# Expert value products on one Trainium2 core: which operand is held, which one passes, and what the last stage has left to turn

## The chip, the cores and the metric

The kernel runs on one core of one Trainium2 chip. The metric is device time in microseconds (us). TensorE (PE) multiplies: a weight load puts a 128x128 tile into its array (the operand that is held), and a matmul passes the columns of the other operand through it into PSUM.
## The reference

One decoder layer for 512 prompt tokens and 64 sample tokens, 2048 wide: a mixer, then a layer that retrieves experts, then a last norm. The change lies behind the mixer. Of the experts it matters that the second table `v_tab` has 128 x 128 rows of 2048, and that the layer adds to each token the sum of 128 chosen rows, each by its weight:

```python
u = u_tab[eidx]
act = jax.nn.gelu(jnp.einsum('thkd,td->thk', u, xb).astype(jnp.float32), approximate=False)
return jnp.einsum('thk,thkd->td', (gate * act).astype(xb.dtype), v_tab[eidx])
...
out = lax.map(one_block, hb).reshape(Tp, D)[:T].reshape(B, L, D)
return x + out.astype(x.dtype)
...
y_prompt = rmsnorm(hp, w_norm_final)
y_sample = rmsnorm(hs, w_norm_final)
```

## The kernel before, in words

The token rows are five tiles: 0 to 3 are the prompt, and tile 4 holds the 64 sample tokens. Tile 0 and tile 4 fetch their chosen expert rows from memory one by one ("gathered"). Tiles 1 to 3, 384 tokens (`ND`), are computed densely: for them every one of the 16384 expert rows is multiplied, with a weight that is zero where an expert was not chosen. Dense products are made in three passes to keep float32 accuracy: each operand is split into a high and a low part, and high x high, high x low and low x high are added up in PSUM.

The stage "hidden" makes the experts' activations from the first table. The stage `outputs` then multiplies the weights (activation times gate) by the second table, and `finish` adds the residual `sums` (what the mixer left) and does the last norm.

In `outputs` the table comes in 128 units of 1 MB (`un`, tiles units_raw, units_whi, units_wlo), eight units to a chunk, 16 chunks. A chunk is 8 x 128 experts; for each chunk the weights of all 384 tokens are loaded (`load_chunk`, two transfers of 1.5 MB, tile units_big), multiplied (`weigh`) and split (`weights_hi`, `weights_lo`; tiles outputs_w_hi and outputs_w_lo, two buffers). The order on every engine is written out by hand in a `body` for two chunks, of which the middle ones run in a hardware loop (`turns`). Per unit j of a chunk:

- SP loads unit n + 2 into one of two raw buffers, once DVE has split unit n. At j = 0 it then issues the next chunk's two weight loads. One queue carries all of these in order.
- ACT splits off the high part of unit n + 1 (L1522), once TensorE is done with unit n - 1. DVE makes the low part (L1526) behind it.
- DVE also weighs the next chunk (L2139, L2146), adds PSUM results to the accumulator `acc` (L2157, L2159), and takes one gathered row (even j) or two (odd j) into `accg` (L2170). POOL issues the gathers into three row buffers.
- PE waits for the low part of unit n, then runs 48 matmuls. The value unit is held, 128 of its columns at a time, and the 384 tokens' weights pass. So a PSUM tile is 128 features x 384 tokens, and `acc` comes out with the features on partitions: transposed.

`finish` therefore loads tiles of `sums`, turns `acc` back with 48 transposes on PE (L2278), adds them on DVE (L2315), and does the norm tile by tile in the order 0, 1, 4, 2, 3: a square with its sum on ACT (L2291), a root (L2293), a Newton step of five small operations on DVE, and the scaling (L2327).

## Time and profile before

| | us |
|---|---|
| median of 3 runs (3772.39 to 3776.6) | 3774.61 |
| the profiled execution's own time | 3772.87 |
| its span in the trace | 3771.1 |
| stage `outputs`, from its first matmul to its last one's end | 2663.9 to 3733.0 |
| `finish`, to the end of the span | 3735.8 to 3771.1 |

The span is what the trace covers, 1.8 us less than the execution's own time. A matmul's duration in the trace is its way through the array, which overlaps with that of the next one; the pace is the distance between two starts.

### The profile page before, as it was taken

The page shows a single profiled execution, that of the slowest core. Times are in us where ns is not written, and L with a number is a line of the kernel's source. Part 1 is how long each engine was busy: PE and PEld are TensorE (multiplying, and loading weights), DVE is VectorE, ACT ScalarE, POOL GpSimd, SP SyncE.
Part 4 walks back from the last instruction along what each step waited for, and adds up shares of the span by engine and source line. Part 5 has one row for each costly group of instructions (what it writes and reads, how often), then busy time and mean ns, then how long its engine had stood idle before and what let it go on. Part 6 is the DMA issues. An engine that isn't in the chain of part 4 may idle for free. (4 is left out here: it accounts for less than half of the span.)

```text
span 3771.1 us, 50107 instructions
## 1 busy us (share of the span) xinstructions
PE 3548.6 (94%) x19479; PEld 3301.7 (88%) x19479; DVE 2556.0 (68%) x3619; ACT 1286.4 (34%) x1610; POOL 920.3 (24%) x609
## 2 busy tenths in 40 slices
PE   8999999776997999999999999999799999999996
PEld 6888887555786878999999999999799999999996
DVE  4112221786323216999999888887889899898987
ACT  5112221332322213323325777774222222222222
POOL 0000000000000000032333333333355445454552
PEclk9999999676998999999999999999899999999998
DMA  5223320542623405487888999999898999989986
GB/s 207 87 111 111 114 106 29 190 148 92 227 90 133 154 35 203 161 327 293 318 332 314 375 372 374 385 372 386 334 376 345 377 362 356 369 350 376 358 344 250
DMA packets 186998, 965.63 MB, mean 256 GB/s; under 512 B 18657, under 2 KB 61345, under 8 KB 86098
## 3 DMA queue, kind: packets, MB, share of 16 engines
q1 hardware_dynamic: 108082, 506.07, 35.6%
q0 software_dynamic: 61264, 426.27, 29.0%
q10 hardware_dynamic: 17488, 31.06, 2.3%
q8 instruction: 108, 1.77, 0.2%
q14 instruction: 56, 0.46, 0.0%
HBM read 865.77 MB, written 97.55 MB: 255 GB/s over the span
## 5 line engine op out<-in xcount | busy, mean ns | idle before, releaser
L1754 PE MATMUL hidden_hp<-dense_hi,units_whi 128*128 128x384 f32 x2048 | 697.4, 341 | 24.1 <-DVE units_wlo L1526 24.1
L1755 PE MATMUL hidden_hp<-dense_lo,units_whi 128*128 128x384 f32 x2048 | 688.0, 336 | 0.0
L1756 PE MATMUL hidden_hp<-dense_hi,units_wlo 128*128 128x384 f32 x2048 | 687.9, 336 | 0.0
L2234 PE MATMUL outputs_vp<-outputs_w_hi,units_whi 128*128 128x384 f32 x2032 | 679.0, 334 | 0.9 <-DVE units_wlo L1526 0.9
L2236 PE MATMUL outputs_vp<-outputs_w_hi,units_wlo 128*128 128x384 f32 x2032 | 678.7, 334 | 0.0
L2235 PE MATMUL outputs_vp<-outputs_w_lo,units_whi 128*128 128x384 f32 x2032 | 678.7, 334 | 0.0
L1522 ACT CAST units_whi<-units_raw 128x2048 fp32r<-128x2048 f32 x214 | 410.7, 1920 | 774.0 <-PE outputs_vp L2236 631.7
L1696 POOL DMA_INDIRECT hidden_row<-u_rows,expert_ids x192 | 360.7, 1878 | 1037.8 <-DVE dots L1977 656.8
L1526 DVE TENSOR_TENSOR units_wlo<-units_raw,units_whi 128x2048 fp32r<-128x2048 f32 x214 | 489.9, 2290 | 117.7 <-ACT units_whi L1522 116.3
L2170 DVE SCALAR_TENSOR_TENSOR accg<-outputs_row,outputs_w_op,accg 128x2048 f32<-128x2048 f32 x192 | 450.8, 2348 | 52.0 <-DMA outputs_row<-v_rows,outputs_id 49.2
L1977 DVE CUSTOM_DVE_ANT_0 hidden_row<-hidden_row,hidden_h_row 128x2048 f32<-128x2048 f32 x192 | 435.7, 2287 | 58.6 <-DMA hidden_row<-u_rows,expert_ids 57.8
L2032 POOL DMA_INDIRECT outputs_row<-v_rows,outputs_id x192 | 320.4, 1669 | 526.4 <-DVE accg L2170 477.8
L1754 PEld LDWEIGHTS hidden_hp<-dense_hi,units_whi 128*128 128x128 f32 x2048 | 387.7, 189 | 29.2 <-DVE units_wlo L1526 28.9
L1755 PEld LDWEIGHTS hidden_hp<-dense_lo,units_whi 128*128 128x128 f32 x2048 | 387.7, 189 | 0.0
L1756 PEld LDWEIGHTS hidden_hp<-dense_hi,units_wlo 128*128 128x128 f32 x2048 | 387.1, 189 | 0.0
L2234 PEld LDWEIGHTS outputs_vp<-outputs_w_hi,units_whi 128*128 128x128 f32 x2032 | 381.4, 188 | 1.9 <-issue 1.2
L2235 PEld LDWEIGHTS outputs_vp<-outputs_w_lo,units_whi 128*128 128x128 f32 x2032 | 381.4, 188 | 0.0
L2236 PEld LDWEIGHTS outputs_vp<-outputs_w_hi,units_wlo 128*128 128x128 f32 x2032 | 381.4, 188 | 0.0
L543 PE MATMUL in_proj_acc<-in_proj_whi,in_proj_rows_hi 128*128 128x512 f32 x960 | 376.2, 392 | 1.9 <-DVE in_proj_wlo L436 1.9
L549 PE MATMUL in_proj_acc<-in_proj_whi,in_proj_rows_lo 128*128 128x512 f32 x768 | 299.5, 390 | 0.0
L548 PE MATMUL in_proj_acc<-in_proj_wlo,in_proj_rows_hi 128*128 128x512 f32 x768 | 299.5, 390 | 0.0
L1828 ACT ACTIVATE hidden_hid<-hidden_hp 128x384 f32<-128x384 f32 x128 | 63.0, 492 | 570.7 <-PE hidden_hp L1756 561.8
(358 smaller groups left out, 4825.2 us busy)
## 6 DMA issues: line engine op xcount, KB each, us to landing
units_raw<-v_units SPq DMA_DIRECT2D x128, 1024.0 KB, 7.2
units_raw<-u_units SPq DMA_DIRECT2D x86, 1024.0 KB, 7.5
in_proj_raw<-w_in SPq DMA_DIRECT2D x48, 1024.0 KB, 5.5
hidden_raw<-u_units SPq DMA_DIRECT2D x42, 1024.0 KB, 7.7
hidden<-hidden_hid SPq DMA_DIRECT2D x128, 192.0 KB, 4.3
gate_mat<-units_big SPq DMA_DIRECT2D x12, 2048.0 KB, 21.6
units_big<-hidden SPq DMA_DIRECT2D x16, 1536.0 KB, 10.1
units_big<-gate_mat SPq DMA_DIRECT2D x16, 1536.0 KB, 15.9
```

The lines of the kernel that those rows point to most:

```text
L543: nc.tensor.matmul(acc[t][:], hi_at(t, kk), whi[q][:, k, :], start=first, stop=False)
L1522: self.nc.scalar.copy(self.hi[s][:], self.raw[raw][:]).then_inc(self.hi_done, 1)
L1526: self.nc.vector.tensor_tensor(self.lo[s][:], self.raw[self.slot(n, s)][:], self.hi[s][:].bitcast(F32), ALU.subtract).then_inc(self.lo_don ...
L1696: pool.indirect_dma_start(row[g % U_ROWS][:], None, u_rows, bass.IndirectOffsetOnAxis(expert_ids[:, g:g + 1], 0)).then_inc(row_in[g % U_RO ...
L1754: mm(o, un.hi[s][:, x, :], h_hi[:, x, :], start=x == 0, stop=False)
L1755: mm(o, un.hi[s][:, x, :], h_lo[:, x, :], start=False, stop=False)
L1756: ins = mm(o, un.lo[s][:, x, :], h_hi[:, x, :], start=False, stop=x == KT - 1)
L1977: v.tensor_tensor_reduce(r[:], r[:], h_row[g % 3 // 2][:], 1.0, 0.0, mult, ALU.add, dots[:, g:g + 1]).then_inc(row_used, 1)
L2170: v.scalar_tensor_tensor(o[:], r[:], w_op[:, j:j + 1], o[:], mult, ALU.add).then_inc(gat.row_used, 1)
L2234: mm(o, un.hi[x][:, at, :], W_hi[s][:, e, :], start=e == 0, stop=False)
L2235: mm(o, un.hi[x][:, at, :], W_lo[s][:, e, :], start=False, stop=False)
L2236: ins = mm(o, un.lo[x][:, at, :], W_hi[s][:, e, :], start=False, stop=e == CH - 1)
```

## The change

The operands of the second table's products change places. The tokens' weights are held (128 tokens x 128 experts), and 512 columns of values pass. A unit is now 4 x 128 experts by 512 features, two units make a group (8 x 128 experts), and each group fills three PSUM tiles, one for each token tile, in token order. DVE adds a group's three tiles in one go at the following even unit. `acc` is three tiles of token rows; they begin as the rows of `sums`, which SP loads at the start of the stage, and the table is laid out anew in memory to match. `finish` has no transposes and no loads of `sums`, and it does the norm in three batches of tiles: 0, then 1 and 2, then 3 and 4. A half of a chunk's weights is now enough for its first unit. The lines shown are the diff without the bookkeeping of names.

```diff
@@ outputs
+        def group(i, s, g):
+            return DS // 2 * (2 * i + s) + g
...
             sp.dma_start(accg[1][0:NSMP, :], sums[SEQ:SEQ + NSMP, :]).then_inc(sums_in, 16)
+            for t in range(VT):
+                sp.dma_start(acc[t][:], sums[P * (t + 1):P * (t + 2), :]).then_inc(acc_in, 16)
             turns(sp, body, T)
-            sp.dma_start(X[:], sums[P:2 * P, :]).then_inc(early, 16)
-            sp.wait_ge(early, 16)
...
-            def add(i, s, j, b):
-
-                k = DT * unit(i, s, j) + b
-                vec.wait_ge(un.done, NKEYS + k + 1)
...
+            def add(i, s, g, t):
+
+                k = VT * group(i, s, g) + t
+                vec.wait_ge(un.done, NKEYS + 2 * VT * group(i, s, g) + VT + t + 1)
+                if isinstance(i, int) and i == s == g == t == 0:
+                    vec.wait_ge(acc_in, 16 * VT)
+
+                wait(vec, added, k + 1 - VT * DS // 2)
+                o = acc[t][:, NB * g:NB * (g + 1)]
+                v.tensor_tensor(o, o, vp[(VT * (DS // 2 * s + g) + t) % 8][:], ALU.add).then_inc(added, 1)
...
-                        add(i, s, j, 0)
+                        if j % 2 == 0:
+                            add_ahead(i, s, j)
                         for x in range(3 * (DS * s + j) // 2, 3 * (DS * s + j + 1) // 2):
                             gathered(i, x)
-                        add(i, s, j, 1)
+                        if is_last(i, s) and j == DS - 1:
+                            for t in range(VT):
+                                add(i, s, DS // 2 - 1, t)
...
-                        for b in range(DT):
-
-                            wait(pe, added, DT * (n - 4) + b + 1)
-                            o = vp[DT * (j % 4) + b][:, 0:ND]
-                            for e in range(CH):
-                                at = DT * e + b
-                                mm(o, un.hi[x][:, at, :], W_hi[s][:, e, :], start=e == 0, stop=False)
-                                mm(o, un.hi[x][:, at, :], W_lo[s][:, e, :], start=False, stop=False)
-                                ins = mm(o, un.lo[x][:, at, :], W_hi[s][:, e, :], start=False, stop=e == CH - 1)
+                        if j < 2:
+                            pe.wait_ge(w_lo_done, 2 * (2 * i + s) + j + 1)
+                        for t in range(VT):
+                            if h == 0:
+
+                                wait(pe, added, VT * group(i, s, j // 2) + t + 1 - 8)
+                            o, at = vp[(VT * (DS // 2 * s + j // 2) + t) % 8], slice(P * t, P * (t + 1))
+                            for e in range(HC):
+                                w = (slice(None), HC * h + e, at)
+                                v_hi, v_lo = (u[x][:, 4 * e:4 * e + 4, :].rearrange("p k f -> p (k f)") for u in (un.hi, un.lo))
+                                mm(o[:], W_hi[s][w], v_hi, start=h == e == 0, stop=False)
+                                mm(o[:], W_hi[s][w], v_lo, start=False, stop=False)
+                                ins = mm(o[:], W_lo[s][w], v_hi, start=False, stop=h == 1 and e == HC - 1)
                             ins.then_inc(un.done, 1)
@@ finish
-        @block.tensor
-        def _(pe):
-            for t in range(1, PTILES):
-                for b in range(4):
...
-                        ins = nc.tensor.transpose(bank[g % 8][:, k, :], acc[:, 4 * b + k, (t - 1) * P:t * P], ident[:])
...
+        batches = [(0, 1), (1, 3), (3, TILES)]
...
-            for n in range(1, TILES):
-                add(order[n])
-                norm(n - 1)
-            norm(TILES - 1)
+            norm(0)
+            add_half()
+            norm(1)
+            norm(2)
@@ kernel
-        "v_units": put("v_units", v.reshape(NCH, CH, NKEYS, DS, DT * P).transpose(0, 3, 2, 1, 4).reshape(NCH * DS, P, D)),
+        "v_units": put("v_units", v.reshape(NCH, 2, CH // 2, NKEYS, D // NB, NB).transpose(0, 4, 1, 3, 2, 5).reshape(NCH * DS, P, D)),
```

On VectorE, units 2 and 3 of the first chunk stood so before. units_wlo is a unit's low part, units_big the weighing of the next chunk, acc the addition of a PSUM tile outputs_vp, and accg a gathered row:

```order
L1526 TENSOR_TENSOR units_wlo1<-units_raw1,units_whi1 128x2048
L2139 TENSOR_TENSOR units_big0<-units_big0,units_big1 128x384 x2
L2157 COPY acc<-outputs_vp4 128x384
L2170 SCALAR_TENSOR_TENSOR accg0<-outputs_row0,outputs_w_op,accg0 128x2048
L2157 COPY acc<-outputs_vp5 128x384
L1526 TENSOR_TENSOR units_wlo0<-units_raw0,units_whi0 128x2048
L2139 TENSOR_TENSOR units_big0<-units_big0,units_big1 128x384 x2
L2157 COPY acc<-outputs_vp6 128x384
L2170 SCALAR_TENSOR_TENSOR accg0<-outputs_row1,outputs_w_op,accg0 128x2048
L2170 SCALAR_TENSOR_TENSOR accg1<-outputs_row2,outputs_w_op,accg1 128x2048
L2157 COPY acc<-outputs_vp7 128x384
```

The same two units with the change:

```order
L1527 TENSOR_TENSOR units_wlo1<-units_raw1,units_whi1 128x2048
L2143 TENSOR_TENSOR units_big0<-units_big0,units_big1 128x384 x2
L2162 TENSOR_TENSOR acc0<-acc0,outputs_vp0 128x512
L2162 TENSOR_TENSOR acc1<-acc1,outputs_vp1 128x512
L2162 TENSOR_TENSOR acc2<-acc2,outputs_vp2 128x512
L2186 SCALAR_TENSOR_TENSOR accg0<-outputs_row0,outputs_w_op,accg0 128x2048
L1527 TENSOR_TENSOR units_wlo0<-units_raw0,units_whi0 128x2048
L2143 TENSOR_TENSOR units_big0<-units_big0,units_big1 128x384 x2
L2186 SCALAR_TENSOR_TENSOR accg0<-outputs_row1,outputs_w_op,accg0 128x2048
L2186 SCALAR_TENSOR_TENSOR accg1<-outputs_row2,outputs_w_op,accg1 128x2048
```

Four additions of 384 columns, one on each side of the gathered rows, became three of 512 columns in the even unit. The last addition of an odd unit, which stood between its gathered rows and the next unit's low part, is gone.

On SyncE, at the start of the stage, these transfers stood one behind the other before:

```order
L2088 DMA accg0<-sums 128x2048
L2089 DMA accg1<-sums 64x2048
L1514 DMA units_raw0<-v_units 128x2048
L1552 DMA units_big0<-hidden 128x3072
L1553 DMA units_big1<-gate_mat 128x3072
L1514 DMA units_raw1<-v_units 128x2048
```

With the change:

```order
L2092 DMA accg0<-sums 128x2048
L2093 DMA accg1<-sums 64x2048
L2095 DMA acc0<-sums 128x2048
L2095 DMA acc1<-sums 128x2048
L2095 DMA acc2<-sums 128x2048
L1515 DMA units_raw0<-v_units 128x2048
L1553 DMA units_big0<-hidden 128x3072
L1554 DMA units_big1<-gate_mat 128x3072
L1515 DMA units_raw1<-v_units 128x2048
```

Three loads of 1 MB now stand ahead of unit 2 (the first units_raw), of the next chunk's weights and of unit 3 (the second units_raw).

## Rows read from the trace of the kernel before

**Rows 1.** Page, costliest groups: a matmul of `outputs`; count, busy, mean ns, idle before

```profile
L2234 PE MATMUL outputs_vp<-outputs_w_hi,units_whi 128*128 128x384 f32 x2032 | 679.0, 334 | 0.9 <-DVE units_wlo L1526 0.9
```

**Rows 2.** Busy time, granted clock (PEclk), DMA share and GB/s by stretch

```profile
core 0: us, PE busy (x) PEld busy (x) DVE busy (x) ACT busy (x) POOL busy (x), PEclk, DMA share, GB/s
2663.90:2674.30 10.40, 10.40 (x48) 10.40 (x49) 7.61 (x9) 3.27 (x2) 0.00 (x0) 0.78 1.02 423
2674.30:3732.80 1058.50, 1057.59 (x6098) 1056.50 (x6096) 949.26 (x729) 282.68 (x156) 533.15 (x374) 1.00 0.90 356
```

**Rows 3.** Timeline of PE, 384 columns: start us, us; 57 starts listed

```profile
2999.70 0.33 PE L2235 MATMUL outputs_vp<-outputs_w_lo,units_whi 128*128 128x384 f32 x1
...
3009.41 0.33 PE L2234 MATMUL outputs_vp<-outputs_w_hi,units_whi 128*128 128x384 f32 x1
```

**Rows 4.** Timeline of PE in the input projection, 512 columns; 28 starts listed

```profile
299.67 0.39 PE L548 MATMUL in_proj_acc<-in_proj_wlo,in_proj_rows_hi 128*128 128x512 f32 x1
...
305.79 0.39 PE L548 MATMUL in_proj_acc<-in_proj_wlo,in_proj_rows_hi 128*128 128x512 f32 x1
```

**Rows 5.** Timeline of ACT at the stage's start; bracket: idle before, and releaser

```profile
2686.19 1.91 ACT L1522 CAST units_whi<-units_raw 128x2048 fp32r<-128x2048 f32 x1 [9.60 <-DMA units_raw<-v_units]
2691.32 1.91 ACT L1522 CAST units_whi<-units_raw 128x2048 fp32r<-128x2048 f32 x1 [3.22 <-PE outputs_vp L2236]
```

**Rows 6.** Timeline of DVE, and DMA use by stretch, at the stage's start

```profile
2688.14 2.29 DVE L1526 TENSOR_TENSOR units_wlo<-units_raw,units_whi 128x2048 fp32r<-128x2048 f32 x1 [3.58 <-ACT units_whi L1522]
...
2664.00:2692.00 28.00, 28.00 (x150) 28.00 (x151) 20.75 (x20) 7.77 (x5) 6.62 (x6) 0.92 1.01 421
```

**Rows 7.** Around a wait of PE in the stage before: timeline row, and stretch behind it

```profile
1741.75 1.11 PE L1713 MATMUL hidden_tq<-ident,units_big 128*128 128x128 f32 x4 [3.69 <-DMA units_big<-queries]
...
1742.00:1746.00 4.00, 4.00 (x15) 4.00 (x15) 3.60 (x8) 2.38 (x2) 0.24 (x1) 0.50 1.02 422
```

**Rows 8.** Timeline of a steady chunk: SP and ACT

```profile
3262.06 0.33 SPq L1514 DMA_DIRECT2D units_raw<-v_units  x1
...
3285.15 1.92 ACT L1522 CAST units_whi<-units_raw 128x2048 fp32r<-128x2048 f32 x1 [8.95 <-DMA units_raw<-v_units]
3290.93 1.92 ACT L1522 CAST units_whi<-units_raw 128x2048 fp32r<-128x2048 f32 x1 [3.86 <-PE outputs_vp L2236]
```

**Rows 9.** Timeline of the same chunk: DVE

```profile
3287.46 2.28 DVE L1526 TENSOR_TENSOR units_wlo<-units_raw,units_whi 128x2048 fp32r<-128x2048 f32 x1
...
3290.60 0.55 DVE L2159 TENSOR_TENSOR acc<-acc,outputs_vp 128x384 f32<-128x384 f32 x1
3291.06 2.34 DVE L2170 SCALAR_TENSOR_TENSOR accg<-outputs_row,outputs_w_op,accg 128x2048 f32<-128x2048 f32 x1
...
3309.51 2.29 DVE L1526 TENSOR_TENSOR units_wlo<-units_raw,units_whi 128x2048 fp32r<-128x2048 f32 x1 [0.59 <-ACT units_whi L1522]
...
3326.15 2.29 DVE L1526 TENSOR_TENSOR units_wlo<-units_raw,units_whi 128x2048 fp32r<-128x2048 f32 x1 [0.77 <-ACT units_whi L1522]
```

**Rows 10.** Waits in the stage: engine line waited for, us in total, times, longest

```profile
ACT units_whi L1522 <- DMA units_raw<-v_units: 129.3, 15, 9.6
DVE accg L2170 <- DMA outputs_row<-v_rows,outputs_id: 49.2, 28, 4.2
```

**Rows 11.** Timeline of DVE in the last unit of `outputs` and in `finish`

```profile
3734.04 0.55 DVE L2159 TENSOR_TENSOR acc<-acc,outputs_vp 128x384 f32<-128x384 f32 x1
...
3743.17 2.27 DVE L2307 TENSOR_TENSOR accg<-accg,finish_half 64x2048 f32<-64x2048 f32 x1
3745.37 0.14 DVE L2321 TENSOR_SCALAR finish_mean<-finish_ss 128x1 f32<-128x1 f32 x1
...
3746.81 2.35 DVE L2327 SCALAR_TENSOR_TENSOR sums<-sums,finish_rstd,finish_w 128x2048 f32<-128x2048 f32 x1
3749.08 2.47 DVE L2315 TENSOR_TENSOR finish_x<-finish_x,finish_t 128x512 f32<-128x512 f32 x4
...
3762.69 2.35 DVE L2327 SCALAR_TENSOR_TENSOR finish_x<-finish_x,finish_rstd,finish_w 128x2048 f32<-128x2048 f32 x1
```

More of the change, by code:

```diff
@@ L61 @@
 DS = D // (DT * P)
+VT = PTILES - 1
 NGATHER = HK + HK // 2
@@ L2038, in wait_row, with outputs @@
         return self.row[j % ROWS]
-def outputs(nc, name, un, big, w_in, v_units, hidden, G, v_rows, expert_ids, dots, acc, accg, sums, X, early):
+def outputs(nc, name, un, big, w_in, v_units, hidden, G, v_rows, expert_ids, dots, acc, accg, sums):
     mult = ALU.mult
@@ L2200, in _ @@
             mm = nc.tensor.matmul
-            def first_unit():
-                for h in range(2):
-                    pe.wait_ge(w_lo_done, h + 1)
-                    for b in range(DT):
-                        o = vp[b][:, 0:ND]
-                        for e in range(HC * h, HC * (h + 1)):
-                            at = DT * e + b
-                            mm(o, un.hi[0][:, at, :], W_hi[0][:, e, :], start=e == 0, stop=False)
-                            mm(o, un.hi[0][:, at, :], W_lo[0][:, e, :], start=False, stop=False)
-                            ins = mm(o, un.lo[0][:, at, :], W_hi[0][:, e, :], start=False, stop=e == CH - 1)
-                        if h == 1:
-                            ins.then_inc(un.done, 1)
             def body(i):
@@ L2218, in body @@
                     for j in range(DS):
-                        n = unit(i, s, j)
+                        n, h, x = unit(i, s, j), j % 2, j % 2
                         un.ready(pe, NKEYS + n)
-                        if j == 0 and not (isinstance(i, int) and i == s == 0):
-                            pe.wait_ge(w_lo_done, 2 * (2 * i + s + 1))
-                        x = j % 2
-                        if isinstance(i, int) and i == s == j == 0:
-                            first_unit()
-                            continue
@@ new lines, in body @@
+                        for t in range(VT):
+                            if h == 0:
[7 more added lines that the diff above has]
+                                ins = mm(o[:], W_lo[s][w], v_hi, start=False, stop=h == 1 and e == HC - 1)
@@ L2302, in _, with add_half @@
             v, d = nc.vector, Steps(vec, dstep)
[L2304 to L2315 removed]
+            def add_half():
+                t = PTILES
+                vec.wait_ge(moved, 1)
+                v.tensor_tensor(X[t][0:NSMP, :], X[t][0:NSMP, :], half[:], ALU.add).then_inc(summed, 1)
@@ L2317, in norm @@
             def norm(n):
[L2318 to L2321 removed]
+                lo, hi = batches[n]
+                at = slice(lo, hi)
+                vec.wait_ge(squared, hi)
+                v.tensor_scalar(mean[:, at], ss[:, at], 1.0 / D, EPS, ALU.mult, ALU.add).then_inc(meaned, 1)
                 vec.wait_ge(meaned, n + 1)
@@ L2323, in norm @@
                 vec.wait_ge(rooted, n + 1)
-                newton_rsqrt(nc, d, rstd[0:R, at], mean[0:R, at], root[0:R, at], tmp[0:R, at])
+                newton_rsqrt(nc, d, rstd[:, at], mean[:, at], root[:, at], tmp[:, at])
                 if n == 0:
                     vec.wait_ge(w_in, 16)
-                v.scalar_tensor_tensor(X[t][0:R, :], X[t][0:R, :], rstd[0:R, at], W[0:R, :], ALU.mult,
-                                       ALU.mult).then_inc(done, 1)
-            for n in range(1, TILES):
-                add(order[n])
-                norm(n - 1)
@@ L2333, in _ @@
-            norm(TILES - 1)
+                for t in range(lo, hi):
+                    R = tile_rows(t)
+                    v.scalar_tensor_tensor(X[t][0:R, :], X[t][0:R, :], rstd[0:R, t:t + 1], W[0:R, :], ALU.mult,
+                                           ALU.mult).then_inc(done, 1)
+            norm(0)
+            add_half()
+            norm(1)
+            norm(2)
 def build(nc, x, w, consts, keys, tables, states, outs):
@@ L2362, in build @@
                            w["norm_ffn"], expert_ids, dots, gates0, G)
-        acc, accg = sb("acc", [P, KT, ND]), [sb(f"accg{x}", [P, D]) for x in range(2)]
-        X, early = sb("sums1", [P, D]), shared.sem("sums_early")
-        outputs(nc, "outputs", un, big, w_in, tables["v_units"], hidden, G, tables["v_rows"], expert_ids, dots, acc, accg, sums, X, early)
-        finish(nc, "finish", ident, sums, w["norm_final"], acc, accg, X, outs["y"])
+        acc, accg = [sb(f"acc{t}", [P, D]) for t in range(VT)], [sb(f"accg{x}", [P, D]) for x in range(2)]
+        outputs(nc, "outputs", un, big, w_in, tables["v_units"], hidden, G, tables["v_rows"], expert_ids, dots, acc, accg, sums)
+        finish(nc, "finish", w["norm_final"], acc, accg, outs["y"])
 def kernel(**inputs):
```

83 lines of the change are left out of this document (32 added, 51 removed).

## Prediction

> **What bounds the kernel now.** I read the page first, then busy time by stretch, then timelines. In `outputs` TensorE is busy from its first matmul to its last: 1057.6 of 1058.5 us at full clock behind the first unit, and its matmuls waited 0.9 us in all for the value units [rows 1, 2]. So the stage's time is the number of matmuls times the distance between two starts. That distance, and not the 334 ns that the page gives as a mean, is the price of a matmul: 57 starts in a row lie 9.71 us apart, 9.71 / 56 = 173.4 ns for 384 columns [rows 3]. 6144 of them make 1065.3 us.
>
> What is close behind matters as much. The DMA engines are busy 0.90 of the stage at 356 GB/s, and VectorE 949.3 of 1058.5 us [rows 2]. Once in each chunk, 15 times, ScalarE waits for a value unit to land and not for TensorE [rows 10]. It is unit 3, which stands in SP's queue behind the next chunk's weights. In the chunk shown it landed at 3285.15, its low part was made from 3287.46 to 3289.74, and TensorE came to it at about 3290.7 (ScalarE is let go at 3290.93, when the last matmul of unit 2 ends, and the next matmul starts some 0.2 us ahead of that end) [rows 8, 9]: 1.0 us to spare. At the stage's start it was 2690.43 against 2691.1 by the same reading, 0.7 us [rows 5, 6].
>
> **Matmuls: -20.8 us.** The change makes 16 chunks x 4 feature blocks x 3 token tiles x 8 x 3 passes = 4608 matmuls of 512 columns in place of 6144 of 384. The columns passed are the same. What falls is what each matmul costs beyond its columns. The trace has 128x512 matmuls of the same types in the input projection, where 28 starts lie 6.12 us apart: 226.7 ns [rows 4]. 4608 x 226.7 = 1044.5 us, against 1065.3. The two prices fit one line of 0.416 ns a column plus 13.5 ns a matmul, and 1536 x 13.5 = 20.8. A unit takes 8.16 us in place of 8.32, a chunk 65.3 in place of 66.6.
>
> The Trainium skill, page "TensorE: Matmul & The Clock Gate", section "Back-to-back issue gap", gives columns / 2.4 + 2.5 ns for an isolated matmul at full clock. By it 512 columns cost 215.8 ns and 384 cost 162.5, and the change would bring 998.4 - 994.4 = 4 us. The rows have 11 ns more at either width, so the trace's prices are taken.
>
> **The loads at the stage's start: +7.4 us, and +1.7 for the clock.** Three loads of 1.05 MB now stand in SP's queue ahead of units 2 and 3. From 2664 to 2692 the DMA engines are full at 421 GB/s [rows 6], so 3.15 MB more push what stands behind by 7.5 us. Unit 3 landed at 2686.2 [rows 5]; it will land near 2693.7, and its low part is there at about 2697.9. TensorE, which started at 2663.9 and needs 10.3 us for the cold first unit and 8.16 for each of the next two, wants it at 2690.5. It waits about 7.4 us, in two parts, because unit 2 stands behind the same loads. Who is queued behind it: nothing but TensorE's own units, since VectorE and ScalarE wait for the same landing. A wait of 3.7 us in the stage before was followed by 4 us at the 1.2 GHz level, with 15 matmul starts where 23 would fit at full pace [rows 7]: 8 x 0.173 = 1.4 us. For one wait of that kind or a little more I take 1.7. Bounds of the whole term: 0, if the gathers give way to the loads and the slack is larger than I read, and 7.4 + 2 x 2 = 11.4.
>
> **The loop through VectorE and the DMA queue: +6 us.** This term decides how much of the gain is kept. From the issue of unit 2 to the landing of unit 3 it is 3262.06 to 3285.15, 23.1 us [rows 8], nearly all full DMA engines. Then 2.0 us for the high part. From the start of unit 3's low part to the end of that of the next chunk's unit 0, which lets SP issue the next unit 2, it is 3287.46 to 3328.44, 41.0 us, with 0.59 + 0.77 us of idle time [rows 9]: 39.6 us of work. The change alters it: ten additions of 384 columns at a cadence of 0.46 us (3290.60 to 3291.06 [rows 9]) become nine of 512 at 0.62 (four in 2.47 [rows 11]), 5.6 for 4.65, so 40.5. The addition ahead of unit 3's low part is gone, so this starts at the high part's end. The loop is then 23.1 + 2.0 + 40.5 = 65.6 us, against 66.6 that TensorE took for a chunk and 65.3 that it will take. What had 1 us to spare now lacks 0.3. The slack of 1.0 us is used up in a few chunks (0.5 of it goes at once, since TensorE gets to unit 3 sooner), and then each chunk waits about 0.3: some 4 us over 12 chunks. Landings scatter by about 1 us from chunk to chunk, and a late one now stops TensorE: 2 more. Bounds: 0, and 1 us in each of 15 chunks, 15 us. VectorE's total is unchanged: a chunk had 16 additions at 0.46 and has 12 at 0.62, 7.4 us either way. The PSUM tiles are no bound: a tile is wanted again eight tiles, over two groups, later.
>
> **The end of the stage: -0.9 us.** VectorE's last addition began at 3734.04, 1.1 us behind the last matmul, because two gathered rows stood ahead of it [rows 11]. Now they come before TensorE is done, and one addition of 0.7 us is left.
>
> **Finish: -7.4 us.** Its first scaling still waits for the norm's weights, so it ends at the same distance, 3743.25, and the sample tile's addition at 3745.44 [rows 11]. Then comes one small chain of 1.44 us (3745.37 to 3746.81), two scalings of 2.35, again 1.44 and two scalings: 3745.37 + 12.3 = 3757.7. Before, the last scaling ended at 3765.04. The two additions of 2.47 us and two of four small chains on the path are gone: 4.94 + 2.9 = 7.8, less half a us of waits that differ. ScalarE's squares (1.9 us each) lie beside the scalings. The transposes stood beside other work and bring nothing.
>
> **Sum.** -20.8 + 7.4 + 1.7 + 6 - 0.9 - 7.4 = -14.0 us against the profiled execution's 3772.87: 3758.9. That execution is 1.7 us below the median of the runs; I split the difference and say 3760.
>
> **The rivals.** (A) The start's loads are hidden and no chunk waits: 3760 - 9.1 - 6 = 3745. For it speaks that both waits hang on 1 us of slack or less, carried over to another schedule; against it, full DMA engines at the start. (B) The loop is dearer, about 1 to 1.9 us a chunk: 3767 to 3782. For it, the rows' landings, for which VectorE already waits 49.2 us, up to 4.2 at once [rows 10]; they stand in the same full stretch. Against it, the DMA engines would be busy 0.90 x 66.6 / 65.3 = 0.92, and idle time makes up for delays. (C) Slower: the wait at a chunk's unit 3 grows to 3.7 us, at which the clock has fallen once [rows 7]. Each such chunk costs 3.7 + 1.7 = 5.4 us; from the forecast, 4 such chunks give 3782 and all 15 give 3841. It decides from a landing 3 us later than now. (D) A matmul of 512 columns costs the same per column here as one of 384, 231.2 ns, and nothing is saved on TensorE: 3781. Only another cost for these operands would do it, as the row of 512 columns says otherwise [rows 4]. By the skill's formula it would be 4 us and not 20.8 that is saved, which gives 3777; it has a share of D's chance.
>
> **How the numbers follow.** Forecast 0.56, with its own range of 3751 to 3767; A 0.15, B 0.17, C 0.05, D and the formula 0.07. A measurement of this kernel can tell about 0.2%, 7.5 us, from no change, so faster means below 3767.1 and slower above 3782.2. The forecast and A are faster but for a little of the upper edge, and B's lower end is too: 0.74. Same takes the rest of B and D: 0.18. Slower is C and the ends of B and D: 0.08. The range of 8 in 10 reaches down to A and up to B's middle: 3745 to 3774.
>
> **What would show it.** Right: starts of 226.7 ns in `outputs`; a first wait of PE for units_wlo of some 7 us in all before unit 3, and the clock at 1.2 GHz behind it; PE waits of 0.2 to 1 us once in a chunk at unit 3; VectorE's waits for ScalarE at units 5 and 7 gone; `finish` 28 us long in place of 35. Wrong: no waits at all (A), PE waits above 1 us in each chunk (B), granted clock below 1.00 in the steady stretch (C), or starts of about 231 ns (D).

## The result, and the profile after

The change made the kernel slower. Median 3806.65 us of 4 runs (3794.0 to 3811.45) against 3775.57 of 4 runs of before (3772.39 to 3776.6): ratio 1.0077, 95% interval 1.006 to 1.0095 (the ratios here and below are worked out from all runs, and can differ a little from that of two medians). The forecast was 3760, and the range ended at 3774. The profiled execution is the lowest of the four, 3794.0 with a span of 3792.2, so the traces explain 21.1 us of span (3792.2 - 3771.1); the 12.7 us from it to the median lie in runs that have no trace. All runs of this document show about the same granted clock, 0.95 to 0.96, but one of e11's ten (3851.53 us at 0.90), which its ratio leaves out; without it e11's median is 3776.98.

The waits of the stage (engine line waited for, us in total, times, longest), to be held against [rows 10]. Of GpSimd's wait for a row buffer, before's line stands first:

```profile
POOL outputs_row L2032 <- DVE accg L2170: 477.8, 103, 14.7
```

```profile
POOL outputs_row L2033 <- DVE accg L2186: 563.7, 133, 14.7
...
ACT units_whi L1523 <- DMA units_raw<-v_units: 263.5, 34, 14.1
DVE accg L2186 <- DMA outputs_row<-v_rows,outputs_id: 67.9, 35, 4.4
...
PE outputs_vp L2236 <- DVE units_wlo L1527: 31.3, 10, 4.5
```

ScalarE waits for a unit's landing 34 times in place of 15, and TensorE, which waited 0.9 us for low parts [rows 1], waits 31.3. Busy time by stretch (columns as in [rows 2]), from the first matmul to unit 3 and from there to the stage's end:

```profile
2667.60:2701.80 34.20, 29.73 (x109) 23.86 (x110) 17.74 (x14) 7.08 (x4) 4.97 (x6) 0.83 1.01 422
2701.80:3762.40 1060.60, 1033.79 (x4501) 851.10 (x4499) 933.89 (x661) 278.82 (x154) 482.73 (x368) 0.99 0.88 348
```

The DMA engines moved 348 GB/s over the long stretch, less than before (356 in [rows 2]), and the granted clock is no longer 1.00. The span's 21.1 us add up so: the stages ahead of `outputs` ended 3.7 us later (2667.6 against 2663.9; this start lay anywhere from 2660.0 to 2670.5 in the runs below and is no effect of the change). From the first matmul to unit 3 it is 34.2 us in place of 27.2, +7.0. From unit 3 to the last matmul's end it is 1060.6 in place of 1041.9 (2691.1 to 3733.0), +18.7. From there to the end of the span it is 29.8 (3762.4 to 3792.2) in place of 38.1, -8.3. Together 21.1.

So the start and the end of the stage can be read off at once (+7.0 and -8.3), and the loss is in the long stretch. One of its chunks, on TensorE:

```profile
3039.61 0.39 PE L2237 MATMUL outputs_vp<-units_wlo,outputs_w_hi 128*128 128x512 f32 x1
...
3042.56 0.39 PE L2238 MATMUL outputs_vp<-units_whi,outputs_w_lo 128*128 128x512 f32 x1
3045.14 0.50 PE L2236 MATMUL outputs_vp<-units_whi,outputs_w_hi 128*128 128x512 f32 x1 [2.19 <-DVE units_wlo L1527]
```

14 starts lie 2.95 us apart, 2.95 / 13 = 226.9 ns, as forecast. Then unit 3's low part is not there. Why it is not shows in the timelines of the same chunk, SP and ACT first, then DVE:

```profile
3015.38 0.33 SPq L1515 DMA_DIRECT2D units_raw<-v_units  x1
...
3040.85 1.91 ACT L1523 CAST units_whi<-units_raw 128x2048 fp32r<-128x2048 f32 x1 [12.27 <-DMA units_raw<-v_units]
```

```profile
3042.79 2.29 DVE L1527 TENSOR_TENSOR units_wlo<-units_raw,units_whi 128x2048 fp32r<-128x2048 f32 x1 [2.71 <-ACT units_whi L1523]
...
3045.94 1.87 DVE L2162 TENSOR_TENSOR acc<-acc,outputs_vp 128x512 f32<-128x512 f32 x3
3047.73 2.34 DVE L2186 SCALAR_TENSOR_TENSOR accg<-outputs_row,outputs_w_op,accg 128x2048 f32<-128x2048 f32 x1
...
3080.69 2.28 DVE L1527 TENSOR_TENSOR units_wlo<-units_raw,units_whi 128x2048 fp32r<-128x2048 f32 x1
```

Issue of unit 2 to landing of unit 3: 25.5 us, where [rows 8] had 23.1. High part 1.9. Start of unit 3's low part to the end of that of the next unit 0: 3042.79 to 3082.97, 40.2, with no idle time. The loop is 67.6 us and TensorE needs 65.3. The fence also shows the new order: three additions in a block (1.87 us), and only then the gathered row. Before, one addition of 0.46 stood there [rows 9].

What a wait leads to is seen behind three of them, the one above and these two:

```profile
2908.09 0.80 PE L2236 MATMUL outputs_vp<-units_whi,outputs_w_hi 128*128 128x512 f32 x1 [4.04 <-DVE units_wlo L1527]
...
3113.83 0.80 PE L2236 MATMUL outputs_vp<-units_whi,outputs_w_hi 128*128 128x512 f32 x1 [3.10 <-DVE units_wlo L1527]
```

Busy time in the 8.2 or 8.3 us behind each, in order of time:

```profile
2908.10:2916.40 8.30, 8.30 (x30) 6.77 (x31) 8.30 (x10) 1.90 (x1) 2.44 (x2) 0.81 0.43 154
...
3045.20:3053.40 8.20, 8.20 (x36) 6.79 (x37) 8.20 (x10) 1.91 (x1) 2.43 (x2) 1.00 0.53 208
...
3113.80:3122.00 8.20, 8.17 (x24) 6.50 (x25) 8.20 (x10) 1.90 (x1) 2.43 (x2) 0.65 0.48 190
```

### The profile page after: what moved, and what is told of

Same layout as the page of the kernel before. It is cut to its first block and busy times, and to the rows that moved or that the text cites. A ratio compares the mean times of both kernels' runs of the same rounds, so it can differ in the third digit from the quotient of the medians.

```text
span 3792.2 us, 46689 instructions
## 1 busy us (share of the span) xinstructions
PE 3538.7 (93%) x17895; PEld 3104.8 (82%) x17895; DVE 2540.0 (67%) x3531; ACT 1286.0 (34%) x1608; POOL 873.5 (23%) x609
## 5 line engine op out<-in xcount | busy, mean ns | idle before, releaser
L2236 PE MATMUL outputs_vp<-units_whi,outputs_w_hi 128*128 128x512 f32 x1536 | 606.0, 395 | 53.8 <-DVE units_wlo L1527 31.3
L2237 PE MATMUL outputs_vp<-units_wlo,outputs_w_hi 128*128 128x512 f32 x1536 | 603.4, 393 | 0.0
L2238 PE MATMUL outputs_vp<-units_whi,outputs_w_lo 128*128 128x512 f32 x1536 | 603.1, 393 | 0.0
L2033 POOL DMA_INDIRECT outputs_row<-v_rows,outputs_id x192 | 338.8, 1765 | 595.6 <-DVE accg L2186 563.7
L2236 PEld LDWEIGHTS outputs_vp<-units_whi,outputs_w_hi 128*128 128x128 f32 x1536 | 292.1, 190 | 119.9 <-DVE units_wlo L1527 36.2
L2237 PEld LDWEIGHTS outputs_vp<-units_wlo,outputs_w_hi 128*128 128x128 f32 x1536 | 292.4, 190 | 60.9
L2238 PEld LDWEIGHTS outputs_vp<-units_whi,outputs_w_lo 128*128 128x128 f32 x1536 | 291.8, 190 | 61.4
```

The lines of the kernel that those rows point to most:

```text
L2236: mm(o[:], W_hi[s][w], v_hi, start=h == e == 0, stop=False)
L2237: mm(o[:], W_hi[s][w], v_lo, start=False, stop=False)
L2238: ins = mm(o[:], W_lo[s][w], v_hi, start=False, stop=h == 1 and e == HC - 1)
```

## The experiments

Fourteen kernels ran, in four groups, each group beside its own runs of before (medians 3775.24, 3777.17, 3774.64 and 3776.0). The legs of the loop are worked out from the timelines of DVE and ACT as in the chunk above, as the mean of 14 chunks. "DMA leg" is the end of unit 0's low part (SP then issues unit 2) to the start of unit 3's high part, "high" from there to the start of its low part, "VectorE" from there to the end of the next unit 0's low part. Rows and SP are the MB that the gathers' queue and SP's moved in the DMA leg; POOL is how long GpSimd waited for a row buffer, and how often; the last column is TensorE's waits for low parts.

```
                                median   ratio, 95%               DMA leg rows SP   high VectorE  chunk  POOL waits  PE waits
before                          3775.57                             23.4  3.82 5.76  2.5   40.8    66.7  477.8, 103    0.9
after                           3806.65  1.0077 (1.0060, 1.0095)    25.5  4.58 5.96  2.0   40.7    68.2  563.7, 133   31.3
e3  no loads at the start       3793.22  1.0041 (1.0027, 1.0055)    26.2  4.69 6.09  1.9   40.5    68.7  563.5, 133   36.7
e4  weights behind unit 3       3831.16  1.0150 (1.0133, 1.0167)    19.9  3.75 3.46  3.3   47.6    70.7  596.8, 130   57.8
e5  gates behind unit 3         3767.83  0.9979 (0.9969, 0.9988)    20.4  3.76 4.59  4.3   41.7    66.4  550.1, 136   13.4
e6  e5, residual last           3771.03  0.9988 (0.9976, 0.9999)    20.2  3.76 4.56  4.1   41.9    66.2  535.2, 132   13.0
e7  short additions             3755.55  0.9946 (0.9930, 0.9963)    23.2  3.97 5.86  2.1   40.1    65.4  508.0,  91    5.8
e8  additions spread            3784.19  1.0021 (1.0010, 1.0031)    25.6  4.66 5.98  2.0   39.8    67.4  470.8, 106   28.0
e9  row, then additions         3775.15  0.9999 (0.9989, 1.0009)    24.5  4.66 5.69  2.0   40.2    66.7  464.4,  91   20.4
e10 e9 and e5                   3754.26  0.9944 (0.9927, 0.9961)    20.1  3.75 4.75  4.3   40.9    65.3  474.1,  89    4.5
e12 e10, residual last          3753.35  0.9942 (0.9925, 0.9959)    20.2  3.71 4.85  4.2   40.9    65.3  478.6,  92    2.1
e11 before, VectorE filled      3778.01  1.0011 (1.0001, 1.0021)    23.3  3.91 5.67  2.6   41.0    66.9  425.8, 108    3.5
e13 before, block ahead of row  3795.50  1.0051 (1.0034, 1.0068)    24.8  4.30 5.90  2.0   40.9    67.6  557.7, 137    8.7
e14 before, row ahead of block  3780.20  1.0012 (1.0002, 1.0021)    24.7  4.64 5.75  2.0   40.4    67.0  477.2,  92    3.7
```

**Are the matmuls cheaper? e1 and e2**: both kernels without the gathered rows, the queue and VectorE relieved.

```diff
@@ POOL
-            turns(pool, body, T)
@@ DVE, gathered
-                v.scalar_tensor_tensor(o[:], r[:], w_op[:, j:j + 1], o[:], mult, ALU.add).then_inc(gat.row_used, 1)
```

> The changed kernel with the gathered rows left out of the stage (neither fetched nor added, so tile 0 and the sample tile lack their experts). It is to price the matmuls alone. Theory of the loop (DMA queue and VectorE at a chunk's start): a third of the DMA bytes and half of VectorE's work are gone, TensorE waits only at the start, starts 226.7 ns apart, from first to last matmul 128 x 8.16 + 2 = 1047 us, up to 1053 with the start's loads. Rival, dearer matmuls in this place: above 1060 us though nothing waits.

> The kernel before with the gathered rows left out in the same way. Both theories: starts 173.4 ns apart, from first to last matmul 128 x 8.32 + 2 = 1067 us. Against e1_no_rows this is the matmul term by itself: 20.5 us between the two stages if the term is right, less than 5 if held weights cost per column what they did.

One run each: 3738.76 and 3777.05. From the first matmul's start to the last one's it is 1046.6 us (e1) and 1067.0 (e2), a difference of 20.4, where the term had 20.8. So the matmuls are cheaper by what was forecast. In after the gain is there too, and waits outweigh it.

**The loads at the start: e3.** The first chunk's results are copied, and the sums are not loaded.

```diff
-            for t in range(VT):
-                sp.dma_start(acc[t][:], sums[P * (t + 1):P * (t + 2), :]).then_inc(acc_in, 16)
...
+                if isinstance(i, int) and i == s == 0:
+                    v.tensor_copy(o, vp[(VT * g + t) % 8][:]).then_inc(added, 1)
```

> The changed kernel without the three loads of the residual at the stage's start: the first chunk's additions are copies, so tiles 1 to 3 lack the residual. Theory of the loop: TensorE reaches unit 3 some 27 us behind its first matmul and not 34, and the time falls by 7 to 8 us; the waits of the later chunks stay. Rival, the loads set off the later waits too (a backlog that is carried on from chunk to chunk): it falls by 20 us or more. Rival, nothing hangs on the loads: within 2 us.

Unit 3 begins 27.3 us behind the first matmul in place of 34.1, so the loads cost 6.8 there. The loop does not get shorter (68.7 us a chunk, PE waits 36.7), and from first to last matmul start the two traces are level, 1094.4 us. The medians lie 13.4 us apart, between the 7 to 8 and the 20 that were given ahead, so the size of the effect on the time stays open (the runs of after alone scatter over 17 us). Either way e3 is slower than before: the loads can explain a part of the loss and not its direction.

**The weights' place in SP's queue: e4 and e5.** The two loads of 1.5 MB for the next chunk stand between units 2 and 3. e4 issues both one unit later, e5 only the second (gate_mat).

```diff
@@ e4
-                        if j == 0 and not is_last(i, s):
+                        if j == 1 and not is_last(i, s):
                             load_w(2 * i + s + 1)
@@ e5
-                        if j == 0 and not is_last(i, s):
-                            load_w(2 * i + s + 1)
+                        if j < 2 and not is_last(i, s):
+                            load_w(2 * i + s + 1, j)
```

> The changed kernel with the next chunk's two weight loads issued one unit later, behind unit 3 in SP's queue and not ahead of it; nothing else. Theory of the loop: unit 3 lands 7 us sooner, the wait at unit 3 goes, VectorE may then wait a little for the weights at unit 2; the time falls by 25 to 40 us, to 3765 to 3780. Rival, the DMA engines' total is the limit: the same bytes, within 5 us. Rival, VectorE's total work is the limit: within 5 us as well.

> The changed kernel with one of the next chunk's two weight loads, that of the gates (gate_mat, 1.5 MB), issued behind unit 3; the other stays ahead of it. Theory of the loop, as the traces of the changed kernel show it (23 to 28 us, on the mean 25.5, from the issue of unit 2 to the landing of unit 3, 1.9 for the high part, 40.2 on VectorE, 68 in all): 1.57 MB fewer ahead of unit 3 are 3.7 to 6.5 us, the loop falls below TensorE's 65.3 us for a chunk, the waits at unit 3 go: 25 to 43 us less than the changed kernel, 3763 to 3780. In the former run with both loads behind unit 3 VectorE stood 5 us a chunk for them; here the queue never runs dry, so it should wait under 1.5. Rival, the DMA engines' total is the limit: within 5 us of the changed kernel, near 3805.

e4 was a miss, 24.5 us above after where 25 to 40 less had been expected, and told something. The DMA leg fell to 19.9 us, but the wait went to VectorE, which now stood before an operand that had not landed, with the low parts of all later units queued behind it:

```profile
DVE units_big L2143 <- DMA units_big<-gate_mat: 69.1, 14, 6.0
```

Its leg grew by 7 us. e5 keeps the first load early, has nearly the same short DMA leg and only 1 us more on VectorE, and gets 38.8 us below after, as expected (VectorE's waits for gate_mat are 3.1 us in all). So what is bought in the queue counts only up to the next operand that is wanted.

**The start's loads once more: e6** is e5 with the residual loaded in the last chunk into the free weight tiles, and added there.

```diff
+                        if j == 0 and is_last(i, s):
+                            sp.wait_ge(w_lo_done, 2 * NCH)
+                            for t in range(VT):
+                                sp.dma_start(spare[t], sums[P * (t + 1):P * (t + 2), :]).then_inc(acc_in, 16)
...
+                v.tensor_tensor(acc[t][:], acc[t][:], spare[t], ALU.add).then_inc(resid, 1)
```

> As e5_gates_behind_unit3, and the residual is not loaded at the stage's start: the first chunk's additions are copies, and in the last chunk, which has no weights to load or to weigh, the three tiles of the residual are loaded into the room of the weights and added by VectorE. Theory: 7 to 9 us less than e5_gates_behind_unit3, 3755 to 3770, below the kernel before. Rival: VectorE's three additions of 2.3 us in the last chunk make TensorE wait, and it is level with e5_gates_behind_unit3.

The stage's first to last matmul start fell by 2.7 us (1069.9 to 1067.2), yet the median is not below e5's, and the intervals overlap; 7 to 9 us less had been expected. The trace shows that the stall moved: in the last chunk unit 3 now stands behind the three residual loads, ScalarE waits 17.26 us for it to land, and TensorE then 7.23 us for its low part (3692.55), the longest wait of its stage.

**How long the additions are: e7, and where they stand: e8.** e7 adds 64 columns of the 512. e8 puts one of the three ahead of the even unit's row, one behind it and one into the odd unit.

```diff
@@ e7
-                o = acc[t][:, NB * g:NB * (g + 1)]
+                o = acc[t][:, NB * g:NB * g + 64]
@@ e8
-                        if j % 2 == 0:
-                            add_ahead(i, s, j)
+                        add_ahead(i, s, j - j % 2, (2,) if j % 2 else (0,))
                         ...
+                        if j % 2 == 0:
+                            add_ahead(i, s, j, (1,))
```

> The changed kernel with each of VectorE's additions cut to 64 of 512 columns (tiles 1 to 3 lack most of the products). It takes VectorE's part of the loop down and leaves DMA alone. Theory of the loop: nine additions in the VectorE leg at 0.2 and not 0.62 us, the leg falls from 40.2 to about 36.5, the loop from 68.2 to 64.4, below TensorE's 65.3, so most of the waits go: 25 to 40 us less than the changed kernel. Rival, DMA's total or the burst alone sets the wait, and VectorE does not: within 5 us.

> The changed kernel with the same three additions of a group, but spread: one ahead of an even unit's gathered row, one behind it, one in the odd unit. Work is the same, only the place differs. Theory of the order (the three additions in a block move the gathers' issues into the stretch in which unit 3 is loaded): the DMA leg goes back to 23.3 us, the loop to about 65, and 30 us or more are won. Theory of the coupling (once the loop is longer than TensorE's chunk, whatever makes it so, the backlog grows into it): no more than the 0.6 us by which the VectorE leg gets shorter, 9 us at most over 15 chunks.

With short additions all of the gain is there, 51 us below after; but this takes work from VectorE and time from ahead of the row together. It did not come the way that was expected either. VectorE's leg was to fall to 36.5 us and stayed at 40.1, now with some 3.9 us of idle time, since a chunk can't be shorter than TensorE's 65.3; what fell is the DMA leg, from 25.5 to 23.2. With the same work in other places, e8 is 22 us below after. That is neither of the figures given ahead of it, but it says that the place is part of the cause. Its DMA leg is as long as after's (25.6); what fell is GpSimd's waits and VectorE's leg.

**The place alone: e9**, the same three additions right behind the row. **e10** joins it with e5.

```diff
-                        if j % 2 == 0:
-                            add_ahead(i, s, j)
                         for x in range(3 * (DS * s + j) // 2, 3 * (DS * s + j + 1) // 2):
                             gathered(i, x)
+                        if j % 2 == 0:
+                            add_ahead(i, s, j)
```

> The changed kernel with one order turned round: in an even unit VectorE takes the gathered row first and then makes the three additions. The same work. It moves the issue of the last gather ahead of unit 2's load from 1.4 to 2.0 us before it to some 3.3 us before it (2.7 in the kernel before, 3.4 in e7_short_additions, where the DMA leg was 23.2 us). Theory of the place (a gather issued right ahead of unit 2 shares the queue's stretch and costs its bytes there): DMA leg 23.5 us, loop 65.7, 25 to 35 us less than the changed kernel, 3770 to 3780. Rival, only idle time of VectorE helps, which spreads all the gathers: the DMA leg stays above 25, less than 10 us are won.

> e9_rows_then_additions and e5_gates_behind_unit3 together. Theory: in e5 the chunk takes 66.4 us because the rows' landings and the gates hold VectorE; the earlier gather takes up to 1 us of that, 3755 to 3765. Rival: VectorE's waits for the gates stay what they are, level with e5 (3768).

Two lines that swap places are worth some 30 us: 31.5 between the medians, 29 by the two ratios, each of which has its own runs of before. The time is as expected, the leg only in part: GpSimd's waits for a row buffer fall from 563.7 to 464.4 us, the DMA leg from 25.5 to 24.5 (23.5 was expected), the chunk from 68.2 to 66.7 (65.7). What went are the long legs. Over the 14 chunks of after they run from 23.2 to 27.6 us, and eight are longer than the longest of e9, where they run from 23.5 to 25.1 (before: 22.4 to 24.9). In e10 the loop takes 65.3 us, what TensorE needs, and of TensorE's idle time only what lies at the start is left (page, costliest groups):

```profile
L2238 PE MATMUL outputs_vp<-units_whi,outputs_w_hi 128*128 128x512 f32 x1536 | 599.7, 390 | 26.9 <-DVE outputs_w_lo L2152 22.3
```

Of the 26.9 us of idle time, 22.3 lie ahead of the stage's first matmul, and 4.5 are the start's wait for unit 2. In after the same row reads:

```profile
L2236 PE MATMUL outputs_vp<-units_whi,outputs_w_hi 128*128 128x512 f32 x1536 | 606.0, 395 | 53.8 <-DVE units_wlo L1527 31.3
```

**Or is it VectorE's lost idle time? e11** leaves before's order and gives VectorE three memsets of 512 columns in each chunk.

```diff
+                        if j in (3, 4, 6):
+                            v.memset(spare[:], 0.0)
```

> The kernel before with three clears of a spare 128x512 tile added to VectorE in units 3, 4 and 6 of each chunk, some 1.3 us a chunk, just about the idle time that it has there; matmuls are as before. If the DMA leg is fixed, the loop is 23.3 + 2.0 + 40.9 = 66.2 us, below TensorE's 66.6, and the time stays within 4 us. If VectorE's idle time is what keeps the gathers apart from unit 2's load, the DMA leg grows to 25 or more, the loop to 68, and the kernel before becomes 15 to 30 us slower, though TensorE has no less time for a chunk than it had.

The DMA leg stayed (23.3), and the time rose by 0.11% (0.01 to 0.21). A VectorE that is fuller by this much does not lengthen the transfers by itself. One of the three fillings stands ahead of the last row that is taken before unit 2's load, but it is 0.48 us long, where the block of after is 1.87.

**All three: e12**, which is e10 with e6's residual.

> e10_rows_first_gates_late with the residual added in the last chunk as in e6_and_residual_last. Theory: 6 us less than e10, 3748 to 3760. Rival: as e6 was level with e5 or 3 us above it, the start's stall only moves, and it is level with e10.

3753.35 us, 0.9942 of before: the best kernel of the study, no different from e10 within the intervals. Its stage takes 1048.7 us from first to last start, 4.9 less than e10's, and as in e6 there is a wait of TensorE in the last chunk, of 2.13 us.

**The order without the change: e13 and e14.** The old matmuls and the old `finish`, but four additions of 384 columns in a block at even units, ahead of the row (e13) or behind it (e14).

```diff
+            def add_ahead(i, s, j):
+                for y in (j - 2, j - 1):
                     ...
+                    for b in range(DT):
+                        add(*back, b)
...
-                        add(i, s, j, 0)
+                        if j % 2 == 0:
+                            add_ahead(i, s, j)
                         for x in range(3 * (DS * s + j) // 2, 3 * (DS * s + j + 1) // 2):
                             gathered(i, x)
-                        add(i, s, j, 1)
```

> The kernel before, its matmuls untouched, with the change's order of additions: at every even unit VectorE adds the last two units' four tiles in a block, ahead of the gathered row. Same additions. TensorE's chunk is 66.6 us. Theory of the place (additions in a block ahead of the row hold back its buffer, POOL asks for the next row later, DMA runs dry in the VectorE leg and has more bytes left for the DMA leg): DMA leg 25 to 26 us in place of 23.4, loop 67.5 to 68.5, 10 to 30 us slower than the kernel before. If the DMA leg is long only because TensorE is faster in the changed kernel: 23.3 + 2 + 40.5 = 65.8 us, below 66.6, and within 4 us of the kernel before.

> As e13_before_in_blocks, with the gathered row first and the block of additions behind it. Theory of the place: the row's buffer comes free as early as it can, DMA leg 23.4 to 24.5, the time within 4 us of the kernel before and 10 us or more below e13. If the place doesn't matter, e13 and e14 are level.

With nothing else of the change, the block ahead of the row makes the kernel before 19.5 us slower (3776.0 to 3795.5), and moving it behind the row takes 15.3 of them back. GpSimd's waits follow the place in all kernels: 535 to 597 us in 130 to 137 waits where a block of full length stands ahead of the row (after, e3 to e6, e13), 464 to 479 in 89 to 92 where it stands behind (e9, e10, e12, e14). The DMA leg doesn't: 24.8 and 24.7 us in e13 and e14, where 25 to 26 and 23.4 to 24.5 had been expected.

## Why the prediction was wrong

**Right.** A matmul costs 226.9 ns at 512 columns, and the whole term measured 20.4 us (e1, e2). The Trainium skill's formula for an isolated matmul (page "TensorE: Matmul & The Clock Gate", section "Back-to-back issue gap") gives 215.8 ns, and an estimate of 4 us saved; the trace does not agree, here as in [rows 3, 4]. The stage's end and `finish` came out at -8.3 us, which is the sum of the two terms; the last addition and the last scaling, to be held against [rows 11]:

```profile
3762.43 0.69 DVE L2162 TENSOR_TENSOR acc<-acc,outputs_vp 128x512 f32<-128x512 f32 x1 [1.87 <-PE outputs_vp L2238]
...
3783.78 2.33 DVE L2312 SCALAR_TENSOR_TENSOR accg<-accg,finish_rstd,finish_w 64x2048 f32<-64x2048 f32 x1
```

The start cost 7.0 us, where 9.1 - 0.5 was forecast; it came as one wait of 4.5 us and 2.5 of half clock (25 starts where 36 fit), not as 7.4 and 1.7:

```profile
2690.91 0.80 PE L2236 MATMUL outputs_vp<-units_whi,outputs_w_hi 128*128 128x512 f32 x1 [4.47 <-DVE units_wlo L1527]
...
2690.90:2699.20 8.30, 8.29 (x25) 6.67 (x26) 4.67 (x3) 1.91 (x1) 3.82 (x4) 0.68 1.00 419
```

VectorE's leg was 40.2 without idle time (forecast 40.5) and the high part 1.9 (forecast 2.0).

**The step that failed** is in the term of the loop: "From the issue of unit 2 to the landing of unit 3 it is 3262.06 to 3285.15, 23.1 us [rows 8], nearly all full DMA engines." That was put into the new loop as it stood, 23.1 + 2.0 + 40.5 = 65.6. It is no constant. The DMA engines are full in this leg, and so its length is the bytes that fall into it, over their rate. Even in before the leg ran from 22.4 to 24.9 us, and TensorE came to unit 3 between 0.05 and 1.35 us behind its low part, 0.76 on the mean of 14 chunks; the forecast took one chunk, with 1.0, and a scatter of about 1 us. With 14 chunks in the mean it grew by 2.1 us, at 0.41 MB a us: the rows' queue had 4.58 MB to move in place of 3.82, SP's 5.96 in place of 5.76. Those 0.96 MB are 2.3 us. They were not moved earlier, in VectorE's leg, where the engines have room. The two windows of before's chunk [rows 8], and those of after's:

```profile
3261.88:3285.15 23.27, 23.27 (x136) 23.27 (x135) 18.32 (x14) 3.83 (x2) 9.20 (x9) 1.00 0.99 408
3285.15:3328.44 43.29, 43.29 (x252) 43.29 (x251) 41.86 (x35) 14.25 (x8) 26.14 (x16) 1.00 0.89 336
```

```profile
3015.38:3040.85 25.47, 25.47 (x114) 21.11 (x113) 19.35 (x11) 3.83 (x3) 10.03 (x10) 1.00 1.00 414
3040.85:3082.97 42.12, 39.93 (x177) 32.72 (x176) 40.11 (x32) 14.25 (x8) 19.12 (x15) 1.00 0.83 315
```

The first stretch is full in both (408 and 414 GB/s). In the second the share falls from 0.89 to 0.83, and 315 GB/s over 42.1 us are 13.3 MB where 336 over 43.3 were 14.6. Most of what is missing are gathered rows (queue, packets, MB, share; second stretch of before, then of after):

```profile
q0 software_dynamic: 1197, 8.76, 54.1%
```

```profile
q0 software_dynamic: 1086, 7.85, 47.6%
```

What the change did to the times at which rows are asked for lies in the order of VectorE. A row's buffer comes free when VectorE has taken the row, and GpSimd asks for the next one only then. Three additions now stand in a block ahead of the row at each even unit where one stood. I counted what the additions cost VectorE (5.6 us for 4.65, right), and not what is queued behind them: the row, GpSimd, a transfer. The order was there to be read. That it is the cause of most of the loss is measured on both sides: with the change (after to e9, some 30 us) and without it (e13 to e14, 15.3 us). That the way goes through GpSimd's waits for row buffers is borne out by their sums, which follow the place; how it reaches the DMA leg is not shown. The swap takes back 1.0 of the leg's 2.1 us, and the rows' bytes in it do not fall: 4.66 MB in e9, 4.58 in after. The rest of the growth is still there in e9, whose loop takes 66.7 us (24.5, 1.9 and 40.2) and whose time is 15 us above the forecast.

**And a size.** With 25.5 + 2.0 + 40.7 = 68.2 us against TensorE's 65.3 a chunk lacks 2.9 us; the forecast had 0.3. Waits of that size were followed by the low clock, rival C's mechanism, which I gave 0.05. It is a quarter of the loss (10.7 of 39 us), and 2.4 us of waiting was enough where I had asked for 3.7. It also lengthens the loop: in the six chunks with a fall VectorE's leg is 41.1 to 42.2 us in place of 40.2, 6.9 us in all, most of it (5.6) idle time in which it waits for ScalarE. So 0.5 of the 2.9 us are not the loop's own. Rival B (a loop dearer by 1 to 1.9 us a chunk, 3767 to 3782) had the right kind of cause and too low an upper end. Its counterargument, "idle time makes up for delays", is the same error: idle time of the DMA engines can be used only while a buffer is free. The slack of 1.0 us ahead of unit 3 was read rightly in the chunk shown, though it is more than the mean, and its smallness is what made the step from hidden to paid so short.

**What stays open.** How the order gets into the DMA leg. It is 23.2 to 23.4 us with before's spread additions (before, e11) and with short ones (e7), and 24.5 to 26.2 in all kernels with additions of full length collected at the even units and both weight loads early, ahead of the row or behind it, spread a little (e8) or not. GpSimd's sum of waits does not tell these apart: e8, e9 and e14 wait as little as before does and still move 4.6 to 4.7 MB of rows in the leg. Nor is the rate in it one number: 0.410 MB a us before and 0.413 in after, but 0.422 in e9 and 0.421 in e14. A leg that is longer also lets one more gather fall into it: in the chunk of after GpSimd issued its last one at 3035.71, 5.1 us ahead of the landing, in before's at 3282.89, 2.3 us ahead. That may be why the leg grows by more than its first cause, but no run separates it. Nor do the traces say why the runs of after scatter over 17 us and those of before beside them over 4. And the swap is worth twice as much with the change as without; that TensorE waits and its clock falls in the one and hardly in the other (31.3 and 8.7 us of waits) is the likely reason, not a shown one.

## What to carry over

A leg in which the DMA engines are full has no fixed length: it is the bytes that other stretches leave to it. A term for it needs the bytes by queue of the whole loop and the time at which each buffer comes free, and it needs them from more than one chunk. When work is gathered into a block on an engine, look first at which buffer release stands behind the block, and put the release ahead of it; here two lines in another order were worth some 30 us, half as much again as the 20.4 us for which the operands were exchanged. And when a fix takes a bound away by 1.3 us a chunk, cost every other loop of that length anew, with bounds as wide as what was never measured.

## What the runs showed of the hardware that was not expected

In the loop of after TensorE's granted clock was below 1.00 in the 8.2 us behind waits of 2.42, 3.10, 3.65, 3.86, 4.04 and 4.11 us, and at 1.00 behind waits of 1.23, 2.19 and 2.19. Each fall cost 1.6 to 2.7 us, as much again as a good part of the wait. This is no threshold. In the same stage of the other kernels the clock fell behind waits of 1.82 us (e5), 1.95 and 2.09 (e6), 2.00 (e4) and 2.14 (e13), and it stayed at 1.00 behind waits of 2.89 to 3.53 us in e3. The length of a wait alone does not tell which it will be. The shortest with a fall (e5) and the longest without (e3), each with the stretch behind it:

```profile
3626.44 0.50 PE L2238 MATMUL outputs_vp<-units_whi,outputs_w_hi 128*128 128x512 f32 x1 [1.82 <-DVE units_wlo L1527]
...
3626.40:3634.60 8.20, 8.16 (x29) 6.55 (x30) 7.80 (x9) 1.90 (x1) 3.12 (x3) 0.79 0.87 348
```

```profile
2762.97 0.50 PE L2235 MATMUL outputs_vp<-units_whi,outputs_w_hi 128*128 128x512 f32 x1 [3.53 <-DVE units_wlo L1527]
...
2763.00:2771.20 8.20, 8.20 (x36) 6.77 (x37) 8.20 (x10) 1.91 (x1) 2.43 (x2) 1.00 0.56 188
```

At the 1.2 GHz level two starts of 512 columns lie 0.43 us apart, less than twice the 0.227 at full clock. It is twice the 0.213 us that 512 columns cost by the prediction's line (0.416 ns a column), so of what a matmul costs beyond its columns nothing is seen at the low level. Two of the stage's first matmuls show it (timeline of PE). The Trainium skill says the same in the section named above, columns / 1.2 at the low level, 426.7 ns, and there the trace agrees.

```profile
2668.16 0.63 PE L2237 MATMUL outputs_vp<-units_wlo,outputs_w_hi 128*128 128x512 f32 x1
2668.59 0.63 PE L2238 MATMUL outputs_vp<-units_whi,outputs_w_lo 128*128 128x512 f32 x1
```
